# Router on unscaled tokens, an earlier gate product and another slot order in a two-layer diffusion backbone

## What is computed

```python
def expert_choice_ffn(h, p):                       # over all tokens of h
    cap = CAPACITY_FACTOR * n // N_EXPERTS         # 2n/16: 32 sample, 16 prompt tokens an expert
    aff = jax.nn.softmax((xs @ p['w_router']).astype(jnp.float32), axis=-1)
    gate, idx = lax.top_k(aff.T, cap)
    xe = xs[idx]
    hg = jnp.einsum('ecd,edf->ecf', xe, p['w_gate'])
    hu = jnp.einsum('ecd,edf->ecf', xe, p['w_up'])
    ye = jnp.einsum('ecf,efd->ecd', jax.nn.silu(hg) * hu, p['w_down']) * gate[..., None]
    ...                                            # scattered back and added up

def trunk_layer(x, cond, p, lam_init, pos, ctx):
    mod = (jax.nn.silu(cond) @ p['w_ada'] + p['b_ada']).reshape(-1, 1, 6 * D_MODEL)
    shift1, scale1, gate1, shift2, scale2, gate2 = jnp.split(mod, 6, axis=-1)
    h = rmsnorm(x, p['norm1']) * (1.0 + scale1) + shift1
    y, own = attention_branches(h, p, lam_init, pos, ctx)
    x = x + gate1 * y
    h = rmsnorm(x, p['norm2']) * (1.0 + scale2) + shift2
    x = x + gate2 * expert_choice_ffn(h, p)
```

## Time and profile before

| | us |
|---|---|
| median of 3 runs | 1977.06 |
| the profiled execution | 1972.57 |
| its span | 1970.8 |
| TensorE busy (matmul) | 1796.6 (91%) |
| VectorE busy | 547.6 (28%) |
| ScalarE busy | 323.2 (16%) |
| GpSimd busy | 106.0 (5%) |
| hardware DMA queue, share of 16 engines | 66.5% |

### The profile page before, as it was taken

How to read it: one execution, slowest core, us unless ns; L and a number is a source line. 1 busy time by engine, 2 the same in 40 slices (tenths; PEclk the granted TensorE clock), 3 DMA queues, 4 the chain that set the end, 5 groups by cost and what they waited for, 6 DMA issues and landing times.

```text
span 1970.8 us, 19069 instructions
## 1 busy us (share of the span) xinstructions
PE 1796.6 (91%) x7788; PEld 870.4 (44%) x7788; DVE 547.6 (28%) x1152; ACT 323.2 (16%) x800; POOL 106.0 (5%) x174
## 2 busy tenths in 40 slices
PE   6999999999998988888789999999998989898876
PEld 3555555654533322322245555566554333332221
DVE  1233225333421212121122341343334222121213
ACT  2232223220310000100022322222112100010001
POOL 0221030000000000000002400300000000000000
PEclk9999999999999999999999999999998999999999
DMA  9136222153799999999941462313527999999996
GB/s 387 72 150 260 98 93 75 65 213 149 298 423 423 424 423 423 423 424 423 423 186 69 173 257 86 118 43 128 213 107 291 423 423 424 423 423 423 424 423 288
DMA packets 78182, 542.70 MB, mean 275 GB/s; under 512 B 9160, under 2 KB 9608, under 8 KB 16400
## 3 DMA queue, kind: packets, MB, share of 16 engines
q1 hardware_dynamic: 76528, 535.65, 66.5%
q0 software_dynamic: 1568, 5.84, 0.8%
HBM read 538.24 MB, written 3.21 MB: 275 GB/s over the span
## 4 chain that ended last, share of the span: by engine, by line
PE 64%; SPq 24%; DMA 5%; DVE 3%; issue 2%; ACT 2%; DVEq 0%
SPq L553 23%; PE banks L1866 13%; PE banks L1501 13%; PE banks L1485 12%; PE banks L1522 6%; DMA arena<-in_w_exp 4%; PE banks L1777 4%; PE banks L1385 3%; PE banks L1931 2%; PE banks L1669 1%; PE banks L1616 1%; PE banks L1730 1%; DMA ring<-in_w_att 1%; PE banks L1437 1%; PE banks L1843 1%
## 5 line engine op out<-in xcount | busy, mean ns | idle before, releaser
L1866 PE MATMUL banks<-ring,arena 128*64 128x512 f32 x1536 | 349.8, 597 | 36.2 <-DMA ring<-in_w_exp 20.0
L1866 PE MATMUL banks<-arena 128*64 128x512 f32 x1536 | 350.4, 596 | 27.6 <-DMA arena<-in_w_exp 21.8
L1501 PE MATMUL banks<-arena,ring 128*128 128x384 f32 x768 | 252.7, 487 | 0.0
L1485 PE MATMUL banks<-ring,arena 128*128 128x384 f32 (+1 forms) x768 | 244.1, 479 | 6.0 <-ACT arena L716 3.9
L1866 PEld LDWEIGHTS banks<-arena 128*64 128x64 f32 x1536 | 105.2, 137 | 258.4 <-issue 179.9
L1866 PEld LDWEIGHTS banks<-ring,arena 128*64 128x64 f32 x1536 | 104.0, 137 | 259.5 <-issue 181.3
L1485 PEld LDWEIGHTS banks<-ring,arena 128*128 128x128 f32 x768 | 146.0, 191 | 100.1 <-ACT arena L716 6.7
L1501 PEld LDWEIGHTS banks<-arena,ring 128*128 128x128 f32 x768 | 145.1, 190 | 98.9 <-issue 1.5
L1329 DVE TENSOR_TENSOR arena<-banks,arena 32x512 f32<-32x512 f32 (+1 forms) x128 | 87.9, 687 | 275.8 <-PE banks L1866 274.4
L1385 PE MATMUL banks<-arena 128*128 128x128 f32 (+3 forms) x740 | 106.6, 277 | 45.6 <-DVE arena L1316 18.6
L1522 PE MATMUL banks<-arena,ring 128*128 128x384 f32 x384 | 129.4, 489 | 2.2 <-ACT arena L773 2.1
(11 more groups left out here) (185 smaller groups left out, 1203.9 us busy)
## 6 DMA issues: line engine op xcount, KB each, us to landing
ring<-in_w_exp SPq DMA_DIRECT2D x192, 1024.0 KB, 26.4
arena<-in_w_exp SPq DMA_DIRECT2D x192, 1024.0 KB, 26.4
ring<-in_w_att SPq DMA_DIRECT2D x80, 1024.0 KB, 7.0
ring<-in_w_att SPq DMA_DIRECT2D x26, 768.0 KB, 8.4
arena<-in_w_att SPq DMA_DIRECT2D x12, 1024.0 KB, 8.8
ring<-in_w_att SPq DMA_DIRECT2D x8, 672.0 KB, 22.1
arena<-gate_rows POOLq DMA_DIRECT2D x4, 1024.0 KB, 5.7
arena<-in_w_vec SPq DMA_DIRECT2D x2, 1024.0 KB, 15.3
```

What stands on the lines that cost most here:

```text
L1485: ins = pe.matmul(ps[:, 0:width], hT[:, k, P * t:P * t + P], slots[n][:, c0:c0 + width], start=k == 0, stop=k == KC - 1)
L1501: ins = pe.matmul(ps[:, 0:TOK], w[:, k, P * (c % 2):P * (c % 2) + P], hT[:, k], start=k == 0, stop=k == KC - 1)
L1866: ins = pe.matmul(PS[64 * h:64 * h + 64, bank], lhs(k), slots[i][:, c0:c0 + BF], start=k == 0, stop=k == KC - 1)
```

## The change

Five edits that hang together:

- Router. The transposes read the residual stream `X` itself, half by half (`x1_half`, `x1_ok`), and no longer the normed tokens. `h2_out` becomes a plain copy of 128x512 on either engine. Scale goes into the router's weights (`WA`, one set for prompt and one for sample, made in the attention stage). Shift becomes a row of 16 logits for each set (`WB`): eight matmuls after the fourth gate of the third mixer, two broadcasting ones after the eighth. The norm's factor multiplies the logits in `affinities`, by one more instruction a tile. On ScalarE `h2_out` now stands ahead of `Sqrt`; on VectorE, for tile 0, `positions_out(0)`, the mask and `h2_out` stand ahead of the norm.
- Second gate. In layer 0 its product and `gain_rows` move ahead of the output projection; in layer 1 the product stays behind it, cut in two around `h2_turn(2)`.
- Slots. In layer 0 the gate's weights keep 8, 9, 10 and 16, the eight modulation units go to `early`, and the experts begin with 8, 9, 10, then `at[4:8]`, 14, then `early`. Layer 1's order of slots is what it was.
- Gathers. The sample gathers of chunks 0 to 3 no longer stand behind `position_turn(1)`: two come before `affinity_turn(1)`, two behind it, with modulation blocks between them in layer 0.
- The gathers, which read the normed tokens, now wait for them by their own semaphore.

The diff, cut to its core:

```diff
             ahead += [(layer + 1, ("ada", 0, k)) for k in range(KC)]
-        turn = [8, 9, 10] + at[0:2] + [15, 11] + at[2:4] + [12, 13] + at[4:8] + [14]
+        early = [at[0], at[1], 15, 11, at[2], at[3], 12, 13]
+        turn = [8, 9, 10] + at[4:8] + [14] + early
+        first = [8, 9, 10] + early + ([] if layer + 1 < DEPTH else at[4:8] + [14])
         alone = ahead.pop(0)
         for n, (of, unit) in enumerate(ahead + [(layer, ("expert", n)) for n in range(ALL_EXP)]):
-            put(of, unit, turn[n % 16])
+            put(of, unit, first[n] if n < len(first) else turn[(n - len(first)) % 16])
             if n == 2:
...
-DVE_LINKS = 107
+DVE_LINKS = 109
 POOL_LINKS = 24
...
         LE = at(o + 796, 2)
+        WA = at(o, 2, KC, NE)
+        WB = at(o + 668, 2, NE)
+        WB2 = at(o + 700, NE)[0:2]
         LAM = at(o + 798, 1)
         LIC = at(o + 799, 2)
-        WARM = at(o + 865, 1)
+        WARM = at(o + 720, 5)
         KPR = at(o + 801, 2, ROPE)
...
         rows_out, gain_out, g1_in, g2_in = sem("rows_out", 32), sem("gain_out", 64), sem("g1_in", 16), sem("g2_in", 16)
-        x1_ok, silu_ok = sem("x1_ok", NT), sem("silu_ok", NE)
+        x1_half, x1_ok, silu_ok = sem("x1_half", NT), sem("x1_ok", NT), sem("silu_ok", NE)
+        shift_mm, shift_ok = sem("shift_mm", 2), sem("shift_ok", 2)
         router_mm, logit_ok, aexp_ok, aff_ok = (sem("router_mm", 2, 1), sem("logit_ok", 2), sem("aexp_ok", 2),
...
             return PS[:, 6 + n % 2 if g + 1 < NG else n]
-
-        def h2_pieces(n):
-
-            t = LATE[n]
-            for c in range(KC):
-                yield c, min(t, 1), P * t, P * t + P, PS[:, 2 * n + c // 4, P * (c % 4):P * (c % 4) + P]
-
-        def h2_dve_chunk(c):
-            return c >= 4
...
                 act.wait_ge(h2_mm.s, h2_mm.at(l, n + 1))
-                for c, s, lo, hi, ps in h2_pieces(n):
-                    if not h2_dve_chunk(c):
-                        ins = nc.scalar.activation(H2[:, c], ps, ACT.Identity, scale=AA[:, 1, s, c:c + 1],
-                                                   bias=MODC[:, s, 24 + c:25 + c])
-                ins.then_inc(h2_act.s, 1)
+                nc.scalar.copy(H2[:, 0:4].rearrange("p c n -> p (c n)"), PS[:, 2 * n]).then_inc(h2_act.s, 1)
...
                         .then_inc(ss_t.s, 1)
+                    h2_out(l, n)
                     act.wait_ge(ms_t.s, ms_t.at(l, n + 1))
...
                     if n >= 1:
-                        nc.scalar.activation(WARM, AA[:, 1, 0, 0:1], ACT.Exp, scale=0.0)
-                    h2_out(l, n)
-                    if n >= 1:
+                        nc.scalar.activation(WARM[:, n:n + 1], AA[:, 1, 0, 0:1], ACT.Exp, scale=0.0)
                         act.wait_ge(logit_ok.s, logit_ok.at(l, n))
...
                     if n == 1:
-                        nc.scalar.activation(WARM, AA[:, 1, 0, 0:1], ACT.Sqrt, scale=0.0)
-
-                nc.scalar.activation(WARM, AA[:, 1, 0, 0:1], ACT.Sigmoid, scale=0.0)
+                        nc.scalar.activation(WARM[:, 0:1], AA[:, 1, 0, 0:1], ACT.Sqrt, scale=0.0)
+
+                nc.scalar.activation(WARM[:, 3:4], AA[:, 1, 0, 0:1], ACT.Sigmoid, scale=0.0)
                 if l + 1 < DEPTH:
...
-                nc.scalar.activation(WARM, AA[:, 1, 0, 0:1], ACT.Sqrt, scale=0.0)
+                nc.scalar.activation(WARM[:, 4:5], AA[:, 1, 0, 0:1], ACT.Sqrt, scale=0.0)
...
                 dve.wait_ge(h2_mm.s, h2_mm.at(l, n + 1))
-                for c, s, lo, hi, ps in h2_pieces(n):
-                    if h2_dve_chunk(c):
-                        ins = nc.vector.tensor_scalar(H2[:, c], ps, AA[:, 1, s, c:c + 1],
-                                                      MODC[:, s, 24 + c:25 + c], ALU.mult, ALU.add)
-                ins.then_inc(h2_dve.s, 1)
+                nc.vector.tensor_copy(H2[:, 4:8].rearrange("p c n -> p (c n)"), PS[:, 2 * n + 1]).then_inc(h2_dve.s, 1)
...
                     gain_scale(l, 1).then_inc(aa_ok.s, 1)
+                    dve.wait_ge(aa_ok.s, aa_ok.at(l, 1))
+                    for s in range(2):
+                        nc.vector.tensor_tensor(WA[:, s], WR, AA[:, 1, s].rearrange("p (k o) -> p k o", o=1)
+                                                .to_broadcast([P, KC, NE]), ALU.mult)
...
                                                op1=ALU.mult).then_inc(ot2_ok.s, 1)
+                dve.wait_ge(shift_mm.s, shift_mm.at(l, 1))
+                nc.vector.tensor_copy(WB2, PS[0:2, 4, 0:NE]).then_inc(shift_ok.s, 1)
                 for c in range(KC):
                     branch(l, ("br2", c))
-
+                    if c == 0:
+                        dve.wait_ge(shift_mm.s, shift_mm.at(l, 2))
+                        nc.vector.tensor_copy(WB, PS[:, 4, 32:32 + 2 * NE].rearrange("p (s e) -> p s e", s=2))\
+                            .then_inc(shift_ok.s, 1)
+
+                def gain_rows():
+
+                    dve.wait_ge(gain_mm.s, gain_mm.at(l, 1))
+                    nc.vector.tensor_tensor(ROW0[:, 0:256], PS[:, 4 if ahead else 3, 0:256], BR[:, BF:BF + 256], ALU.add)\
+                        .then_inc(gain_row.s, 1)
+
+                ahead = l + 1 < DEPTH
                 dve.wait_ge(g1_in.s, g1_in.at(l, 16))
                 nc.vector.memset(AFT, 1.0)
+                if ahead:
+                    gain_rows()
                 def residual(i):
...
                         ins = nc.vector.tensor_tensor(x, x, TMP[:, h], ALU.add)
+                        ins.then_inc((x1_half, x1_ok)[h].s, 1)
                         if (i, h) == (1, 0):
                             h2_out(l, 0)
-                    ins.then_inc(x1_ok.s, 1)
+                    if i == 2:
+                        positions_out(0)
+                        dispatch_part(0, 1, 2).then_inc(early_ok.s, 1)
+                        h2_out(l, 2)
...
                     lg, st, rs = LG[:, t0:t0 + nt], ST[:, t0:t0 + nt], RS[:, t0:t0 + nt]
-                    link(nc.vector.reduce_max(st, ps, AX), l)
+                    for n in range(nt):
+                        ins = nc.vector.scalar_tensor_tensor(out=lg[:, n], in0=ps[:, n], scalar=rs[:, n:n + 1],
+                                                             in1=WB[:, 1 - i], op0=ALU.mult, op1=ALU.add)
+                    link(ins, l)
+                    link(nc.vector.reduce_max(st, lg, AX), l)
                     top = st.rearrange("p (t o) -> p t o", o=1).to_broadcast([P, nt, NE])
-                    nc.vector.tensor_tensor(lg, ps, top, ALU.subtract).then_inc(logit_ok.s, 1)
+                    nc.vector.tensor_tensor(lg, lg, top, ALU.subtract).then_inc(logit_ok.s, 1)
                     dve.wait_ge(aexp_ok.s, aexp_ok.at(l, i + 1))
...
                 residual(2)
-                positions_out(0)
-                dispatch_part(0, 1, 2).then_inc(early_ok.s, 1)
-                h2_out(l, 2)
-                dve.wait_ge(gain_mm.s, gain_mm.at(l, 1))
-                nc.vector.tensor_tensor(ROW0[:, 0:256], PS[:, 3, 0:256], BR[:, BF:BF + 256], ALU.add)\
-                    .then_inc(gain_row.s, 1)
+                if not ahead:
+                    gain_rows()
                 affinities(1)
...
-                pe.wait_ge(xn_t.s, xn_t.at(l, n + 1))
-                for c, _, lo, hi, ps in h2_pieces(n):
-                    ins = settle(turn(ps, XN2[:, lo // P, P * c:P * c + P]))
+                pe.wait_ge(x1_half.s, x1_half.at(l, n + 1))
+                for c in range(KC):
+                    if c == 4:
+                        pe.wait_ge(x1_ok.s, x1_ok.at(l, n + 1))
+                    ins = settle(turn(PS[:, 2 * n + c // 4, P * (c % 4):P * (c % 4) + P],
+                                      X[:, LATE[n], P * c:P * c + P]))
                 ins.then_inc(h2_mm.s, 1)
...
                 for k in range(KC):
-                    ins = pe.matmul(PS[:, bank, col:col + NE], H2[:, k], WR[:, k],
+                    ins = pe.matmul(PS[:, bank, col:col + NE], H2[:, k], WA[:, min(t, 1), k],
                                     start=k == 0, stop=k == KC - 1)
...
                         ins.then_inc(sqd_mm.s, 1)
+                    if c == 3:
+                        pe.wait_ge(aa_ok.s, aa_ok.at(l, 1))
+                        for k in range(KC):
+                            ins = pe.matmul(PS[0:2, 4, 0:NE], MODC[:, :, 24 + k], WR[:, k], start=k == 0, stop=k == KC - 1)
+                            if k == 0:
+                                settle(ins)
+                        ins.then_inc(shift_mm.s, 1)
+                pe.wait_ge(shift_ok.s, shift_ok.at(l, 1))
+                for s in range(2):
+                    ins = settle(pe.matmul(PS[:, 4, 32 + NE * s:32 + NE * s + NE], IDT[0:2, s:s + 1].to_broadcast([2, P]),
+                                           WB2, start=True, stop=True))
+                ins.then_inc(shift_mm.s, 1)
                 pe.wait_ge(msd_ok.s, msd_ok.at(l, 1))
...
+                def gain(first, last):
+
+                    for k in range(first, last):
```

(34 more changed lines are left out.)

## The result

The changed kernel has a median of 1986.59 us (8 runs, 1982.85 to 1990.03), the kernel before, on the same chip, 1977.82 us (8 runs, 1972.81 to 1980.27). The ratio is 1.0051 with a 95% interval of 1.0035 to 1.0066: slower, outside the forecast range.

A forecast was written before the change was run, and what follows sets the result against it. Expert stages were taken as bound by the DMA weight stream, the part ahead by TensorE. Gains of 4.3 us (layer 0) and 1.3 us (layer 1) made 5.6, so 1977.06 us became 1971.5, range 1966 to 1979.5.

The forecast's parts named there:

- (e): Layer 1 from x1 to experts: 5.85 us saved by router and split gathers, start 2.9 late, net gain 2.9 us.
- What would show it: Signs to check in the trace, among them three expert units issued near 470 and layer 1's first release near 1505.
- (a): Layer 0 slots and gate product: four transfers leave the unbroken stream, 9.9 us; the product costs 2.4 us before the projection.
- (d): Layer 0 summed: projection's last slot release 5.6 us later, against 9.9 us from transfers; gain 4.3 us.
- (b): Shift logits, both layers: 20 extra TensorE instructions cost 1.5 us (1.1 to 2.5); waiting for the shift row costs nothing.
- (c): Second tile's copy, root and scaling form a loop: router 1.0 us later, projection ends 1.4 us late (0.4 to 2.7).
- rival 2: ScalarE's table load falls in the square root's path for every tile, 7.8 us more: 1979.3 us; chance 0.10.
- (f): Clock falls ahead of layer 1's prompt gathers, costing 1.6 us; layer 1's gain becomes 1.3 us.
- Rival 4: Split gathers bring nothing because another engine holds layer 1's prompt gathers: 1972.8 us; chance 0.09.
- Rivals 2 and 3: Rival 3: layer 0's early loads are held until the projection frees slots, 7.4 us stay: 1978.9 us; chance 0.06.
- rival 1: Clock stays up in layer 1 because gate product, router and gathers follow each other: gain 7.2, 1969.9 us; chance 0.20.
- wrong if: Refuting signs: gaps within an expert stage's stream, last projection slot's release moving over 9.9 us, or differing attention stages.

The follow-up runs named there:

- the kernel that has it alone: Kernel before with only layer 1's later slot rounds in the changed order (8, 9, 10, at[4:8], 14, early): 1990.76 us, ratio 1.0083.
- Layer 0's part alone: Kernel before with layer 0's gate product ahead of the output projection and layer 0's new slot order; router, gathers, layer 1 as before: 1971.53 us, ratio 0.9963.
- Root first: The mended change with ScalarE taking the second tile's square root ahead of its copy of the transposes: 1968.94 us, ratio 0.9966.
- the filler: The mended change plus three unread 128x512 matmuls ahead of layer 1's last position transpose: 1968.07 us, ratio 0.9961.
- the mended change: The changed kernel with only layer 1's later slot rounds put back in the old order (8, 9, 10, early, at[4:8], 14): 1971.32 us, ratio 0.9973.
- root first and filler: The mended change with both the second tile's root ahead of the copy and three unread matmuls in layer 1: 1968.52 us, 0.9949; again on another chip, 0.9965.

## Why the prediction was wrong, point by point

**The step that failed** is a sentence that I did not work out: "Layer 1's order of slots is what it was", in the description of the change, and with it the first release near 1505, two us behind the experts, in (e) and in "What would show it". I read `first` for layer 1, which is the old order, and not what `turn` now does for its second round. It has no term in the sum and no rival. It is worth 17.0 us in D (15.9 in the kernel that has it alone), three times my whole forecast gain. I had written myself that in layer 1 the queue stands still until the first expert unit is used; what was missing was the question which unit the next issue waits for. With that one line mended the ratio is 0.9973, and the forecast was 0.9972 (1971.5 of 1977.06 us). The agreement of the total is partly luck, as the terms below show, and that of the medians (1971.32 us) wholly so, as they come from different chips.

**(a) and (d), layer 0.** The early units were issued where I put them. The gate product cost 2.4 us: from third branch to projection it is 471.80 - 447.37 = 24.43 us after, 465.58 - 443.53 = 22.05 before. Rows of after:

```profile
446.82 0.61 PE L1790 MATMUL banks<-arena 2*128 2x16 f32 x4
447.37 20.91 PE L1536 MATMUL banks<-arena,ring 128*128 128x384 f32 x64
468.20 3.66 PE L1475 MATMUL banks<-arena 128*32 128x256 f32 x64
471.80 20.87 PE L1813 MATMUL banks<-ring,arena 128*128 128x512 f32 x48
...
508.95 1.93 PE L1424 MATMUL banks<-arena 128*128 128x16 f32 x16 [0.73 <-DVE arena L962]
```

The projection's last slot is released 5.7 us later from the anchor (505.66 + 16.15 - 210.52 against 499.44 + 14.21 - 208.03), forecast 5.6. The four transfers were sized at 9.9 us; with A 3.9 us shorter they brought 3.9 + 5.7 = 9.6. Layer 0's part alone says the same: SyncE's group of four ends there at 518.08, 3.2 us later from the anchor, and 6.4 + 3.2 = 9.6. Gain of layer 0 in all: 3.9 us, forecast 4.3.

**(b) Shift logits.** From anchor to third branch: 447.37 - 210.52 = 236.85 us, before 443.53 - 208.03 = 235.50: 1.35 us, forecast 1.5. The new wait for the copied row costs nothing, as said.

**(c) The square root's loop.** Right in kind: TensorE idles ahead of the second router, released by VectorE's copy. 0.73 us instead of 1.0; with the longer router chain the projection took 48.16 us (471.80 to 519.96) against 47.15 before, 1.0 us more where I had 1.4. The order on both engines for the second tile in after, layer 1, is the one I wrote down (ScalarE's copy, root, table load; VectorE's reciprocal, token scaling, copy):

```profile
1471.92 0.59 ACT L720 COPY arena<-banks 128x512 f32<-128x512 f32 x1 [3.49 <-PE banks L1396]
1472.40 0.21 ACT L868 ACTIVATE arena<-arena 128x1 f32<-128x1 f32 x1
1472.63 1.28 ACT L870 ACT_TABLE_LOAD   x1
```
```profile
1472.64 0.16 DVE L1222 RECIPROCAL arena<-arena 128x1 f32<-128x1 f32 x1 [4.03 <-ACT arena L868]
1472.84 0.75 DVE L1223 TENSOR_SCALAR arena<-arena 128x1024 f32<-128x1024 f32 x1
1473.51 0.68 DVE L962 COPY arena<-banks 128x512 f32<-128x512 f32 x1
```

The table load stands behind the root, not in the loop, so rival 2 did not happen. For the first tile the load does stand between copy and root (494.18 to 495.46 us in layer 0), but the first router followed the projection's matmuls without a wait. Root first removes the wait and brings A 0.95 us.

**(e) Layer 1 up to the gathers.** First prompt gather from the anchor: 1498.83 - 1215.80 = 283.03, before 1505.37 - 1218.83 = 286.54: 3.5 us earlier, forecast 2.9. **(f) The clock.** This is the term that was mis-sized. Rows of after, layer 1:

```profile
1498.04 0.20 PE L1396 MATMUL banks<-arena 16*128 16x16 f32 x1 [3.06 <-DVE arena L1258]
1498.83 1.90 PE L1884 MATMUL banks<-arena 128*128 128x64 f32 x8 [0.59 <-DVE arena L1272]
...
1505.78 3.65 PE L1902 MATMUL banks<-ring,arena 128*64 128x512 f32 x16
```

I took it that the clock rises in the middle of the gathers, so that 3.3 us of work cost 1.6 more. It stayed at 0.50 until nearly the last of them (0.50 from 1500 to 1505 us, 0.92 from 1505 to 1510): 6.95 us against 1508.98 - 1505.37 = 3.61 before, 3.3 us. That eats the 3.5: forecast 2.9 - 1.6 = 1.3 us, measured 3.5 - 3.3 = 0.2. In the trace with the root first the clock rose within the gathers, and they took 5.67 us (1500.62 to 1506.29): the size of this term is not fixed by the kernel's text. The Trainium skill (TensorE: Matmul & The Clock Gate, Why this matters for your kernels), which asks for matmul bursts without long idle gaps, was borne out more fully than I allowed: the 3.06 us gap ahead of the position transpose shrinks to 0.48 with the filler, and C by 3.2 us.

**The rivals.** Rival 4, that the split gathers bring nothing, is what happened to layer 1, by another mechanism than the one I gave: no engine held the prompt's gathers; the clock took back what the split had saved. Rivals 2 and 3 did not happen, nor did rival 1 without filler. Of my "wrong if" list the first item held: the stream has a gap within the expert stage, at 1505 to 1525 us.

**What the parts are worth.** Layer 0's slots and gate product: 0.9963. Router rewrite, folded norm and split gathers: 0.9996, since their shift logits and the loop cost layer 0 what they save in layer 1. No run shows the reworked router to pay in the time of the whole kernel: without filler 0.9973 with it and 0.9963 without it, on different chips; with filler, on one chip, 0.9965 and 0.9958 (the stretches of one trace each have it ahead by 1.6 us there).

## What to carry to other kernels

Where one queue issues all loads in a written order, ask of every change to a slot plan which *use* the next issue waits for, in each round and each layer: an order that is right for the round in which it was planned can block the next round, and TensorE stays busy meanwhile, so the loss shows as empty DMA windows and as a late landing at the end, not as idle time where it arises. A saving ahead of a stretch in which TensorE has been idle is worth only what the clock leaves of it; price it from a row at the low level for the whole stretch that follows. And split a program with two similar layers into stretches with anchors before you compare: a trace of the same kernel moved by 3 us in its start-up and by over 1 us between the layers, while the stretches that carried the change repeated within 0.2 us.

## What the runs showed of the hardware that I had not expected

The stretches B (228.7 to 233.4 us) and E (18.9 to 21.9 us) vary between traces, and one kernel traced twice had 232.09 and 233.44 in B. The same 14 matmuls stand at the end of each layer, behind an equal pause of 2.9 us. Here they are at the end of layer 0, in the mended change, with the root first, and twice in the kernel with root first and filler:

```profile
992.14 5.39 PE L1974 MATMUL banks<-arena 128*128 128x256 f32 x14 [2.94 <-issue]
```
```profile
989.99 8.45 PE L1977 MATMUL banks<-arena 128*128 128x256 f32 x14 [2.95 <-issue]
```
```profile
988.11 7.09 PE L1980 MATMUL banks<-arena 128*128 128x256 f32 x14 [2.94 <-issue]
```
```profile
990.97 8.44 PE L1980 MATMUL banks<-arena 128*128 128x256 f32 x14 [2.95 <-issue]
```

From 988 to 1000 us the first had a clock of 1.00, the second 0.72. These 14 account for all that E varies (5.39 us of them in before, 8.45 in after: the 3.0 us of the table), and with a later group of 96 matmuls of 128x336 (28.64 us in the first trace, 30.33 in the second, from 1015.26 and 1016.17 on) for all that B varies. Of the 16.8 us between the spans of after and before, 12.9 are A, C and D, 3.0 are E, -1.6 are B and 2.5 the start-up. Whether the edits have a part in the last three no run settles.

So after a pause of about 3 us the clock may be up or down for the next several us, and one and the same program had 7.09 and 8.44 us at one place. And filler is no free remedy: issued when the clock is already down, three matmuls took 5.33 us instead of 2.74 and delayed what they were to speed up.
